# Where scores, turns and splits stand between the projections of a three-layer block (one core)

## The chip, the core and the metric

The kernel runs on one core of a Trainium2 chip. The core has five engines that work side by side: TensorE (PE) multiplies matrices into PSUM, VectorE (DVE) and ScalarE (ACT) work elementwise, GpSimd (POOL) too, SyncE (SP) issues DMAs. Each engine takes its own instructions strictly in order; between engines they wait on semaphores. The metric is the device time of one execution in microseconds.

## The reference

The input is 256 tokens of 1024 floats. `first_block` is a layer with two attentions over the same projection and a feed-forward; `second_block` has two layers, each with an attention, a mixture of 32 experts and a gated embedding. What matters here, cut:

```python
# first_block
proj = einsum(rms_norm(h), w_in); qa, ka, va, c_q, c_kv, k_rope = split(proj)
qa, ka = rms_norm(per head)                    # 8 heads of 64
out_a = dilated_attention(qa, ka, va, rel_bias)
qb = einsum(rms_norm(c_q), w_uq)               # 8 heads of 96, "latent" heads
kv = einsum(rms_norm(c_kv), w_ukv)             # keys' part and values
qb, kb = rms_norm(per head), then rope
out_b = causal_block_attention(qb, kb, vb)
h = h + concatenate([out_a, out_b]) @ w_o
h = h + square(relu(rms_norm(h) @ w_ff1)) @ w_ff2
# second_block, layer 0: nsa_attention (16 heads, with compressed blocks), experts, gate
# second_block, layer 1: moba_attention
k, v = split(rms_norm(h) @ w_kv_shared); k = rms_norm(k)        # 4 heads
q = rms_norm(rms_norm(h) @ w_q)                                 # 16 heads
o = softmax(q k + alibi) v; h = h + o @ w_out
h = h + hier_moe(rms_norm(h))
h = h + sigmoid(rms_norm(h) @ ple_w_gate) * (p @ ple_w_proj)    # the end
```

## The kernel before

**Tiling.** The 256 tokens are two tiles of 128 (`t`). All matrices are float32; a weight chunk is split into a rounded high part (ScalarE, `split`, line 906) and a low remainder (VectorE, line 909), and each product is three matmuls: high by high, high by low, low by high (`pe_linear`, line 888). A chunk has two of the eight 128-row blocks of a matrix, up to 512 columns wide. Four split chunks fit (`PAIRS`), so `take_linear` splits chunk n + 4 while TensorE works on chunk n; at the end of a column group it takes the result out of its bank (lines 933 to 937), with the normalization's factor.

**Order of work.** Nothing is scheduled by a planner: each engine's order is the order of the calls in its block (`@block.tensor`, `.scalar`, `.vector`, `.gpsimd`, `.sync`), written by hand. `pe_linear` has a hook, `ahead`, which issues other work before chunk c of its first group.

**A head's way.** A projection's result is squared (`squares`, ScalarE), summed (VectorE), a root is taken (`act_root`, ScalarE), refined by six short VectorE instructions (`dve_root`, lines 749 to 754), and the heads are scaled (`scale_heads`, line 957, on VectorE or GpSimd). TensorE turns them (`pe_turn`, line 792) and ScalarE and VectorE take the turned heads to SBUF (`take_turn`). Then `scores_of_pair` (line 970) scores two heads, VectorE adds mask or bias and finds the maximum (`bias_head`, 1090), ScalarE takes the exponential (`exps_of`, 1054), TensorE turns the probabilities (995), one of the two copies them, TensorE multiplies with the values (1006), and `mix_core` (1119) scales four heads at once. Banks 0 to 3 hold scores and projections, 4 and 5 turned probabilities, 6 and 7 values.

**Names.** `l_uq`, `l_ukv`, `l_va` are the projections of the latent queries, of the latent keys and values, and of the first attention's values; `t_a`, `t_b` the turns of the first and of the latent attention's heads (qa/ka and qb/kb); `att_a`, `att_b`, `att_n`, `att_m` the four attentions. Before the first matmul of `l_va` TensorE waits for `dve_scaled` 2, both scalings of the first attention's heads. The feed-forward (`pe_in` 1336, `pe_down` 1346) adds 32 units into four banks; `dve_units` then adds the banks to `h` (1438). In the last layer before: `l_q` (all 16 query heads), `l_k`, `l_v`, and after each half of the queries its squares, sum, root and scaling; `t_mq[0]`, `t_mq[1]`, `t_mk` are the turns of the query halves and the keys. The kernel ends with `l_gate[1]`, sigmoid (933), product and addition (1970, 1973), and two stores.

## Time and profile before

| | us |
|---|---|
| three runs | 1069.54, 1071.67, 1073.91 |
| their median | 1071.67 |
| the profiled execution | 1069.12 |
| its span, first to last instruction | 1067.3 |
| TensorE busy | 1016.9 (95%) |
| VectorE busy | 762.6 (71%) |
| ScalarE busy | 701.4 (66%) |
| GpSimd busy | 104.5 (10%) |
| mean granted TensorE clock | 0.994 |

Busy times overlap, since the engines work side by side. A timeline row gives the start in us from the span's start, the length of the merged instructions, engine, line and operation; in brackets stands how long the engine was idle before, and whose work ended that. The profiled execution is one execution, 0.2% below the median.

### The profile page before, as it was taken

What the parts mean: (1) busy time and instruction counts of PE and PEld (TensorE: products, weight loads), DVE (VectorE), ACT (ScalarE), POOL (GpSimd) and SP (SyncE); (2) the same over time, 40 slices, a digit from 0 to 9 for tenths busy, and PEclk for the clock granted to TensorE, in tenths of its full rate; (3) what the DMA queues carried; (4) which work ended last, traced back from release to release, by engine and by line L of the source; (5) the groups of instructions that cost most, each with busy time, mean ns of one, the idle gap of its engine ahead of it and who ended that gap; (6) DMA issues with size and microseconds to landing.
All of it is one profiled execution on the core that took longest, in us unless ns stands there. A gap on an engine that the chain in (4) does not pass through costs nothing.

```text
span 1067.3 us, 17403 instructions
## 1 busy us (share of the span) xinstructions
PE 1016.9 (95%) x6109; PEld 849.7 (80%) x6109; DVE 762.6 (71%) x1338; ACT 701.4 (66%) x1201; POOL 104.5 (10%) x194
## 2 busy tenths in 40 slices
PE   7997899999999999999899999999989999999998
PEld 6875878999998777887687877867878688877866
DVE  4686557666665675877668887887777668888876
ACT  5665535444444545765599898957576588899955
POOL 9008000000000100200510000000000330000000
PEclk9999999999999999999999999999999999999999
DMA  9972027666663557004449999854314429899941
GB/s 293 294 226 72 1 79 230 185 194 183 185 185 122 178 171 245 23 2 158 177 159 335 325 342 336 303 178 152 126 73 158 178 98 326 327 338 337 339 167 40
DMA packets 106157, 209.25 MB, mean 196 GB/s; under 512 B 7737, under 2 KB 51745, under 8 KB 105825
## 3 DMA queue, kind: packets, MB, share of 16 engines
q1 hardware_dynamic: 103584, 204.04, 56.0%
q0 software_dynamic: 2064, 3.25, 1.1%
q8 instruction: 43, 0.70, 0.3%
q10 hardware_dynamic: 432, 0.99, 0.3%
q14 instruction: 34, 0.27, 0.1%
HBM read 207.19 MB, written 1.06 MB: 195 GB/s over the span
## 4 chain that ended last, share of the span: by engine, by line
PE 84%; DVE 7%; ACT 4%; issue 2%; DMA 1%; SPq 0%; ACTq 0%; POOL 0%; DVEq 0%; POOLq 0%
PE bank L888 22%; PE bank L1663 18%; PE bank L1682 11%; PE bank L1336 8%; PE bank L1346 8%; PE bank L1006 4%; PE bank L970 2%; PE bank L792 2%; PE bank L995 2%; PE bank L1704 1%; PE bank L1531 1%; DMA ring<-in_a_w_in 1%; PE bank L1674 1%; PE bank L1493 1%; PE bank L2166 1%
## 5 line engine op out<-in xcount | busy, mean ns | idle before, releaser
L888 PE MATMUL bank<-weight_parts,x_high 128*128 128x512 f32 (+2 forms) x768 | 224.9, 377 | 8.6 <-ACT x_high L856 2.6
L1663 PE MATMUL bank<-expert_high,block_high 128*128 128x256 f32 x560 | 184.1, 329 | 3.4 <-ACT block_low L1611 2.4
L1591 DVE TENSOR_TENSOR expert_low<-expert_w,expert_high 128x1024 fp32r<-128x1024 f32 x140 | 164.7, 1219 | 6.9 <-ACT expert_high L1584 6.6
L888 PEld LDWEIGHTS bank<-weight_parts,x_high 128*128 128x128 f32 x768 | 139.9, 189 | 35.9 <-ACT x_high L856 7.0
L909 DVE TENSOR_TENSOR weight_parts<-ring,weight_parts 128x1024 fp32r<-128x1024 f32 (+3 forms) x112 | 122.1, 1110 | 51.9 <-ACT weight_parts L906 51.3
L1663 PE MATMUL bank<-expert_high,block_low 128*128 128x256 f32 x560 | 158.2, 282 | 0.0
L1663 PE MATMUL bank<-expert_low,block_high 128*128 128x256 f32 x560 | 158.0, 282 | 0.0
L906 ACT CAST weight_parts<-ring 128x1024 fp32r<-128x1024 f32 (+3 forms) x112 | 104.3, 956 | 78.0 <-PE bank L888 60.0
L1584 ACT CAST expert_high<-expert_w 128x1024 fp32r<-128x1024 f32 x140 | 140.1, 1052 | 17.1 <-DMA expert_w<-in_moe_w_up 16.5
L888 PE MATMUL bank<-weight_parts,x_low 128*128 128x512 f32 (+2 forms) x384 | 143.7, 374 | 0.0
L1682 PE MATMUL bank<-expert_w,junk 128*128 128x512 f32 x280 | 131.3, 592 | 0.0
L1663 PEld LDWEIGHTS bank<-expert_high,block_high 128*128 128x128 f32 x560 | 106.8, 191 | 19.6 <-issue 14.8
L1663 PEld LDWEIGHTS bank<-expert_low,block_high 128*128 128x128 f32 x560 | 106.8, 191 | 15.3 <-issue 15.3
L1663 PEld LDWEIGHTS bank<-expert_high,block_low 128*128 128x128 f32 x560 | 106.8, 191 | 0.0
L1336 PE MATMUL bank<-x_high,parts 128*128 128x256 f32 x512 | 97.5, 283 | 0.4 <-DVE x_low L858 0.3
L1346 PE MATMUL bank<-parts,hid_parts 128*128 128x512 f32 x384 | 92.9, 391 | 0.0
L1738 DVE SCALAR_TENSOR_TENSOR arena<-bank,home_w,arena 128x1024 f32 x64 | 82.2, 1284 | 9.1 <-issue 5.3
L1336 PEld LDWEIGHTS bank<-x_high,parts 128*128 128x128 f32 x512 | 82.1, 191 | 2.2 <-issue 0.7
L888 PEld LDWEIGHTS bank<-weight_parts,x_low 128*128 128x128 f32 x384 | 72.5, 189 | 12.9
L1346 PEld LDWEIGHTS bank<-parts,hid_parts 128*128 128x128 f32 x384 | 70.1, 188 | 13.3
L1682 PEld LDWEIGHTS bank<-expert_w,junk 128*128 128x128 f32 x280 | 47.7, 190 | 34.4 <-issue 34.4
L1609 ACT CAST block_high<-sorted_high 128x1024 fp32r (+1 forms) x70 | 73.4, 1051 | 1.8 <-issue 1.0
(362 smaller groups left out, 1683.4 us busy)
## 6 DMA issues: line engine op xcount, KB each, us to landing
expert_w<-in_moe_w_gate SPq DMA_DIRECT2D x70, 512.0 KB, 5.8
expert_w<-in_moe_w_up SPq DMA_DIRECT2D x70, 512.0 KB, 7.2
expert_w<-in_moe_w_down SPq DMA_DIRECT2D x70, 512.0 KB, 5.3
ring<-in_w_ff SPq DMA_DIRECT2D x64, 512.0 KB, 3.9
ring<-in_w_in SPq DMA_DIRECT2D x16, 512.0 KB, 8.1
ring<-in_a_w_in SPq DMA_DIRECT2D x16, 512.0 KB, 6.5
ring<-in_ple_w_gate SPq DMA_DIRECT2D x16, 512.0 KB, 5.6
ring<-in_w_o SPq DMA_DIRECT2D x8, 512.0 KB, 4.1
```

What stands on the lines that cost most here:

```text
L888: mm = nc.tensor.matmul(bank[:, j["m"] % 4, 0:n], j["operand"][x][:, 2 * c + kk, at[0]:at[1]], weight_parts[:, number % PAIRS, w, kk * n:( ...
L906: nc.scalar.copy(high, raw_weights).then_inc(weights_high, 1)
L909: nc.vector.tensor_tensor(low, raw_weights, high, ALU.subtract).then_inc(weights_split, 1)
L1006: mm = nc.tensor.matmul(bank[:, 6 + t, (n % 4) * P:(n % 4 + 1) * P], probT[:, n % 2, q * P:(q + 1) * P], v[:, kt, at - 64:at + 64], start= ...
L1336: mm = nc.tensor.matmul(bank[:, b, 0:256], parts[:, u % 2, w, k * P:(k + 1) * P], x[:, k, :], start=k == 0 and n == 0, stop=k == KB - 1 an ...
L1346: mm = nc.tensor.matmul(bank[:, 2 * t + half, :], hid_parts[:, u % 2, x, t * P:(t + 1) * P], parts[:, u % 2, w, 2048 + half * 512:2048 + ( ...
L1584: nc.scalar.copy(half_of(expert_high[:, b % 2, :], j), half_of(expert_w[:, b % DEPTH, 0:2048], j)).then_inc(ex_cast, 1)
L1591: nc.vector.tensor_tensor(half_of(expert_low[:, b % DEPTH, 0:2048], j), half_of(expert_w[:, b % DEPTH, 0:2048], j), half_of(expert_high[:, ...
L1609: nc.scalar.copy(block_high[:, b % 2], sorted_high[:, :, ds(at, P)]).then_inc(ex_copied, 1)
L1663: mm = nc.tensor.matmul(bank[:, 4 + b % 2, 0:256].rearrange("p (q n) -> p q n", q=2), x[:, b % 2, k, :], w[:, k], start=k == 0 and n == 0, ...
L1682: mm = nc.tensor.matmul(bank[:, 2 * (b % 2) + half, :], hidTs[:, b % 2, :], expert_w[:, b % DEPTH, 2048 + half * 512:2048 + (half + 1) * 5 ...
L1738: v.scalar_tensor_tensor(out=here, in0=bank[:, 2 * (b % 2):2 * (b % 2) + 2, :].rearrange("p b n -> p (b n)"), scalar=share_of, in1=here, o ...
```

## The change

1. **First attention.** `t_a` is still turned before chunk 2 of `l_va`; the first pair of heads is now scored before chunk 3, and VectorE adds the biases of the first two heads before it takes `l_va`. VectorE does the splits and the taking of `l_uq[2:]` ahead of the scaling of qa, and those of `l_ukv[:2]` ahead of the scaling of ka. The latent queries' root is taken earlier, ahead of the turns.
2. **All attentions by four.** The start is written out anew, with scores in pairs, each pair waiting for its own two banks.
3. **Latent attention.** Heads are turned pair by pair, queries and keys alternating; the first two jobs stand ahead of the wait for the mix, and scores wait for their own pair.
4. **Feed-forward end.** VectorE adds the first token tile once `first_tile_down` is there, which the last unit's first six matmuls set.
5. **Compressed attention.** VectorE inverts the gates ahead of taking the compressed scores.
6. **Last layer's projections.** Order: first half of the queries (`l_mq0`), keys, second half (`l_mq1`), values; turns and first scores stand inside the values' projection, the turn of the second half inside the attention's start.
7. **End.** The last gate projection's second half is two groups of 256 columns; the output goes in six stores.

The diff, cut:

```diff
+        if halved_end:
+            wide += [256, wide.pop() - 256]
...
-    t_b = turn_heads(vb_q, 8, qbT, None) + turn_heads(vb_k, 8, kbT, None)
+    t_b = [job for i in range(0, 8, 2) for view, dest in ((vb_q, qbT), (vb_k, kbT))
+           for job in turn_heads(view[:, :, i:i + 2], 2, dest[:, i:i + 2], None)]
...
-    l_q = linear(a["b_w_q_2"][0], KB, D_MODEL, x_parts, moba_q, "copy", n_moba)
     t_kv = turn(h, KB, [(kv_high, gains["kv_norm"], kv_low)])
+    l_mq0 = linear(a["b_w_q_2"][0], KB, 512, x_parts, moba_q, "copy", n_moba, at=0)
     l_k = linear(a["w_kv_shared_2"], KB, 256, (kv_high, kv_low), moba_kv, "copy", n_moba, at=0)
+    l_mq1 = linear(a["b_w_q_2"][0], KB, 512, x_parts, moba_q, "copy", n_moba, at=512)
     l_v = linear(a["w_kv_shared_2"], KB, 256, (kv_high, kv_low), moba_kv, "copy", n_moba, at=256)
-    run(l_q + l_k + l_v)
-    r_mq = [root(16, DIM), root(16, DIM)]
-    r_mk = root(8, DIM)
+    run(l_mq0 + l_k + l_mq1 + l_v)
...
-        if n >= 4:
-            pe.wait_ge(biased, n)
-        scores_of_pair(pe, n, four[0:2])
-        scores_of_pair(pe, n + 2, four[2:4])
-
-    def pe_attention(pe, s, compressed=False, by_four=False, before_values=None, scored=2):
+        for pair in (0, 2):
+            if n >= 4:
+                pe.wait_ge(biased, n + pair - 2)
+            scores_of_pair(pe, n + pair, four[pair:pair + 2])
...
+                    if j % 2 == 0:
+                        wait_turned(pe, turned_by[j:j + 2])
...
+        if free is not None:
+            turn_probs(first)
+            free()
         if scored == 2:
             scores_of_pair(pe, first + 2, here[2:4])
-        turn_probs(first)
-        for j in range(len(here)):
+        if free is None:
+            turn_probs(first)
+        pe.wait_ge(biased, first + 2)
+        scores_of_pair(pe, first + 4, here[4:6])
+        turn_probs(first + 1)
+        if between is not None:
+            between()
+        pe.wait_ge(biased, first + 4)
+        scores_of_pair(pe, first + 6, here[6:8])
+        if before_values is not None:
+            before_values()
+        values(first, here[0])
+        for j in range(1, len(here)):
             if j % 4 == 0 and j + 4 < len(here):
                 scores_of_four(pe, first + j + 4, here[j + 4:j + 8])
             if j + 1 < len(here):
                 turn_probs(first + j + 1)
             if compressed and j == len(here) - 2:
                 pe_turn_compressed(pe)
-            if j == 0 and before_values is not None:
-                before_values()
             values(first + j, here[j])
...
+            if u == UNITS - 1 and t == 0:
+                mm.then_inc(first_tile_down, 1)
...
-        dve.wait_ge(down_made, OPEN + UNITS)
-        for t in range(TILES):
+        for t in range(TILES):
+            if t == 0:
+                dve.wait_ge(first_tile_down, 1)
+            else:
+                dve.wait_ge(down_made, OPEN + UNITS)
...
-            sp.wait_ge(ple_done, 7 + t)
-            sp.dma_start(out[0, t * P:(t + 1) * P, :], h[:, t, :]).then_inc(stored, 16)
-        sp.wait_ge(stored, 32)
+        for done, cols in ((5, slice(0, 512)), (7, slice(512, 768)), (9, slice(768, 1024))):
+            for t in range(TILES):
+                sp.wait_ge(ple_done, done + t)
+                sp.dma_start(out[0, t * P:(t + 1) * P, cols], h[:, t, cols]).then_inc(stored, 16)
+        sp.wait_ge(stored, 96)
...
+        def first_pair_of_a():
+            wait_turned(pe, t_a)
+            wait_took(pe, l_ukv)
+            scores_of_pair(pe, att_a["first"], att_a["heads"][0:2])
+
+        pe_linear(pe, l_va, ahead={2: lambda: pe_turn(pe, t_a), 3: first_pair_of_a})
         wait_took(pe, l_va)
-        scores_of_pair(pe, att_a["first"], att_a["heads"][0:2])
         pe_attention(pe, att_a, by_four=True)
         pe.wait_ge(pool_scaled, 2)
         pe.wait_ge(*probT_of(att_b["first"] - 1))
         pe.wait_ge(*probT_of(att_b["first"] - 2))
+        pe_turn(pe, t_b[:2])
         pe.wait_ge(mixed, att_b["first"] // 4)
-        pe_turn(pe, t_b)
-        wait_turned(pe, t_b)
-        pe_attention(pe, att_b)
+        pe_turn(pe, t_b[2:])
+        pe_attention(pe, att_b, turned_by=t_b)
...
-        pe_linear(pe, l_q[0:2], t_moba)
-        pe_turn(pe, t_kv)
-        pe_linear(pe, l_q[2:4])
+        pe_linear(pe, l_mq0, t_moba, ahead={2: lambda: pe_turn(pe, t_kv)})
         pe_linear(pe, l_k, t_kv)
-        pe.wait_ge(dve_scaled, 4)
-        pe_linear(pe, l_v, ahead={2: lambda: pe_turn(pe, t_mq[0])})
-        pe.wait_ge(dve_scaled, 5)
-        pe_turn(pe, t_mq[1])
-        pe.wait_ge(pool_scaled, 5)
-        pe_turn(pe, t_mk)
-        wait_turned(pe, t_mk + t_mq[0] + t_mq[1])
-        wait_took(pe, l_v)
-        scores_of_pair(pe, att_m["first"], att_m["heads"][0:2])
-        pe_attention(pe, att_m, by_four=True)
+
+        def turn_keys_of_m():
+            pe.wait_ge(pool_scaled, 5)
+            pe_turn(pe, t_mk)
+
+        def turn_first_heads():
+            pe.wait_ge(dve_scaled, 4)
+            pe_turn(pe, t_mq0)
+
+        def first_pair_of_m():
+            wait_turned(pe, t_mk + t_mq0)
+            wait_took(pe, l_mq1)
+            scores_of_pair(pe, att_m["first"], att_m["heads"][0:2])
+
+        def turn_last_heads():
+            pe.wait_ge(dve_scaled, 5)
+            pe_turn(pe, t_mq1)
+
+        pe_linear(pe, l_mq1)
+        pe_linear(pe, l_v, ahead={1: turn_keys_of_m, 2: turn_first_heads, 3: first_pair_of_m})
+        pe_attention(pe, att_m, by_four=True, between=turn_last_heads, before_values=lambda: wait_turned(pe, t_mq1),
+                     free=lambda: wait_took(pe, l_v))
...
+        take_linear(dve, l_uq[2:], "dve")
         dve.wait_ge(scale_ready, 1)
         scale_heads(v, qa, scales(r_a, 0, 8), dve_scaled)
-        take_linear(dve, l_uq[2:], "dve")
+        take_linear(dve, l_ukv[:2], "dve")
         scale_heads(v, ka, scales(r_a, 8, 8), dve_scaled)
+        take_linear(dve, l_ukv[2:], "dve")
         dve.wait_ge(squared, 2)
         v.tensor_reduce(r_bq["sum"], flat_mix[:, 0:1536].rearrange("p (h d) -> p h d", d=96), AX.X,
                         ALU.add).then_inc(sums_ready, 1)
-        take_linear(dve, l_ukv, "dve")
+        dve_root(dve, r_bq, scale_ready)
         take_turn(dve, t_a, "dve")
         dve_latent_sums(dve)
+        dve.wait_ge(toep_ready, 32)
+        for i in range(2):
+            bias_head(dve, att_a["first"] + i, att_a["heads"][i])
         take_linear(dve, l_va, "dve")
-        dve_root(dve, r_bq, scale_ready)
+        for i in range(2, 4):
+            bias_head(dve, att_a["first"] + i, att_a["heads"][i])
         dve_root(dve, r_bk, scale_ready)
-        dve.wait_ge(toep_ready, 32)
-        dve_attention(dve, att_a, by_four=True)
+        dve_attention(dve, att_a, by_four=True, begun=4)
...
+        take_linear(dve, l_k, "dve", between={2: scale_first_half})
+        dve.wait_ge(squared, 8)
         v.tensor_reduce(r_mk["sum"], work[:, 0:512].rearrange("p (h d) -> p h d", d=64), AX.X,
                         ALU.add).then_inc(sums_ready, 1)
         dve_root(dve, r_mk, scale_ready)
-        take_turn(dve, t_mq[0], "dve")
+        take_linear(dve, l_mq1, "dve")
+        take_turn(dve, t_mk, "dve")
+        dve.wait_ge(squared, 9)
+        v.tensor_reduce(r_mq1["sum"], rows[:, 1, :].rearrange("p (h d) -> p h d", d=64), AX.X,
+                        ALU.add).then_inc(sums_ready, 1)
+        take_turn(dve, t_mq0, "dve")
+        dve_root(dve, r_mq1, scale_ready)
+        for i in range(2):
+            bias_head(dve, att_m["first"] + i, att_m["heads"][i])
+        dve.wait_ge(scale_ready, 8)
+        steepen(r_mq1, 8, 8)
         take_linear(dve, l_v, "dve")
-        take_turn(dve, t_mq[1], "dve")
-        take_turn(dve, t_mk, "dve")
-        dve_attention(dve, att_m, by_four=True)
+        scale_heads(v, mq[:, :, 8:16, :], scales(r_mq1, 0, 8), dve_scaled)
+        for i in range(2, 4):
+            bias_head(dve, att_m["first"] + i, att_m["heads"][i])
+        dve_attention(dve, att_m, by_four=True, begun=4, later=lambda: take_turn(dve, t_mq1, "dve"))
```

What it moves, as the programs list it. VectorE ahead of the values' projection of the first attention (`weight_parts_49` are the split weights, `ring` the raw ones; `arena` holds the projection, `stat` the roots). Before, then now:

```order
L957 TENSOR_TENSOR arena<-arena,stat 128x512 [waits scale_ready]
L957 TENSOR_TENSOR arena<-arena,stat 128x512
L909 TENSOR_TENSOR weight_parts_49<-ring,weight_parts_49 128x1024 [waits weights_high] x3
L937 TENSOR_SCALAR arena<-bank,stat 128x256 [waits rooted,lin_made]
L957 TENSOR_TENSOR arena<-arena,stat 128x512 x2
L2493 TENSOR_REDUCE stat<-mix 128x16 [waits squared]
L909 TENSOR_TENSOR weight_parts_49<-ring,weight_parts_49 128x1024 [waits weights_high]
L937 TENSOR_SCALAR second<-bank,stat 128x512 [waits rooted,lin_made]
```

```order
L914 TENSOR_TENSOR weight_parts_49<-ring,weight_parts_49 128x1024 [waits weights_high] x3
L944 TENSOR_SCALAR arena<-bank,stat 128x256 [waits rooted,lin_made]
L964 TENSOR_TENSOR arena<-arena,stat 128x512 [waits scale_ready]
L964 TENSOR_TENSOR arena<-arena,stat 128x512
L914 TENSOR_TENSOR weight_parts_49<-ring,weight_parts_49 128x1024 [waits weights_high]
L944 TENSOR_SCALAR second<-bank,stat 128x512 [waits rooted,lin_made]
L964 TENSOR_TENSOR arena<-arena,stat 128x512 x2
L914 TENSOR_TENSOR weight_parts_49<-ring,weight_parts_49 128x1024 [waits weights_high]
```

The scaling of the queries moved behind three splits and a take, that of the keys behind a fourth split and a second take; the sum over `mix` comes later still.

TensorE at the start of the last attention (`kv_high`, `kv_low` are the keys' and values' input, `ring` the turned heads, `work` the probabilities, `arena` the heads to be turned). Before, from the turns behind the last chunk of `l_v`:

```order
L792 MATMUL bank<-table,arena 128x128 [waits dve_turned,act_turned,dve_scaled]
L792 MATMUL bank<-table,arena 128x128 x3
L792 MATMUL bank<-table,arena 128x128 [waits dve_turned,pool_scaled]
L970 MATMUL bank<-ring 128x128 [waits act_took,dve_took,dve_turned,act_turned]
L970 MATMUL bank<-ring 128x256 x2
L995 MATMUL bank<-table,work 128x128 [waits act_probT,probs_made]
L970 MATMUL bank<-ring 128x128 [waits biased]
L995 MATMUL bank<-table,work 128x128 [waits dve_probT,probs_made]
L1006 MATMUL bank<-arena,probT 128x128 [waits mixed,act_probT]
```

And now, from the first scores, ahead of the last chunk:

```order
L977 MATMUL bank<-ring 128x128 [waits act_took,dve_took,dve_turned,act_turned]
L977 MATMUL bank<-ring 128x256 x2
L893 MATMUL bank<-weight_parts_49,kv_high_57 128x256 [waits weights_split]
L1002 MATMUL bank<-table,work 128x128 [waits act_probT,probs_made]
L977 MATMUL bank<-ring 128x128 [waits dve_took,act_took]
L977 MATMUL bank<-ring 128x128 [waits biased]
L1002 MATMUL bank<-table,work 128x128 [waits dve_probT,probs_made]
L797 MATMUL bank<-table,arena 128x128 [waits dve_turned,act_turned,dve_scaled]
L977 MATMUL bank<-ring 128x128 [waits biased]
L1013 MATMUL bank<-arena,probT 128x128 [waits act_probT,mixed,dve_turned,act_turned]
```

The first scores moved in front of a chunk of the values' projection, the keys' turns (which wait for `pool_scaled`) three chunks ahead, and the last turns (those that wait for `dve_scaled`) behind three pairs of scores.

## Rows read from the trace of the kernel before

**Rows 1.** The page, chain of waits by engine.

```profile
PE 84%; DVE 7%; ACT 4%; issue 2%; DMA 1%; SPq 0%; ACTq 0%; POOL 0%; DVEq 0%; POOLq 0%
```

**Rows 2.** TensorE's waits, 60 to 96.5; columns: engine, line, releaser, total, times, longest.

```profile
PE bank L888 <- ACT second L935: 1.5, 1, 1.5
PE bank L888 <- DVE arena L937: 1.0, 1, 1.0
```

**Rows 3.** VectorE's timeline; columns: start, us, engine, line, operation.

```profile
75.11 3.49 DVE L909 TENSOR_TENSOR weight_parts<-ring,weight_parts 128x1024 fp32r<-128x1024 f32 x3
78.51 0.48 DVE L937 TENSOR_SCALAR arena<-bank,stat 128x256 f32<-128x256 f32 x1
78.91 1.28 DVE L957 TENSOR_TENSOR arena<-arena,stat 128x512 f32<-128x512 f32 x2
```

**Rows 4.** ScalarE's timeline, the same stretch.

```profile
79.07 1.49 ACT L2248 ACTIVATE mix<-arena 128x1536 f32<-128x1536 f32 x1 [3.51 <-issue]
80.47 1.03 ACT L906 CAST weight_parts<-ring 128x1024 fp32r<-128x1024 f32 x1
```

**Rows 5.** TensorE's timeline, values' projection and start of the first attention.

```profile
82.22 0.70 PE L888 MATMUL bank<-weight_parts,x_high 128*128 128x512 f32 x2 [1.52 <-ACT second L935]
...
84.40 0.73 PE L888 MATMUL bank<-weight_parts,x_high 128*128 128x512 f32 x2 [0.55 <-DVE second L937]
...
96.95 1.58 PE L970 MATMUL bank<-ring 64*128 64x128 f32 x16 [0.99 <-DVE arena L937]
102.12 0.55 PE L995 MATMUL bank<-table,work 128*128 128x128 f32 x3 [3.59 <-ACT work L1054]
...
105.92 1.19 PE L1006 MATMUL bank<-arena,probT 128*128 128x128 f32 x6
```

**Rows 6.** Windows of 2 us; the third number from the end is the granted clock.

```profile
102.00:104.00 2.00, 1.78 (x13) 1.39 (x15) 0.71 (x6) 2.00 (x10) 2.00 (x3) 0.81 0.04 8
104.00:106.00 2.00, 2.00 (x13) 1.35 (x11) 0.64 (x4) 1.94 (x9) 2.00 (x2) 0.50 0.00 0
...
784.00:786.00 2.00, 1.60 (x10) 0.88 (x9) 1.92 (x13) 1.37 (x7) 0.00 (x0) 0.52 0.00 0
```

**Rows 7.** Timelines of GpSimd and of VectorE, the same moment.

```profile
96.08 2.50 POOL L2071 TENSOR_TENSOR arena<-second,gain_bk 128x512 f32<-128x512 f32 x2
...
97.42 1.20 DVE L751 TENSOR_TENSOR stat<-stat 128x16 f32<-128x16 f32 x1
```

**Rows 8.** TensorE's timeline, start of the latent attention.

```profile
115.92 3.67 PE L792 MATMUL bank<-table,arena 128*96 128x128 f32 x32 [1.06 <-DVE mix L1119]
120.42 0.46 PE L986 MATMUL bank<-ring 96*128 96x128 f32 x2 [0.83 <-ACT ring L833]
```

**Rows 9.** Timelines of TensorE and of VectorE, end of the feed-forward.

```profile
338.56 5.63 PE L1346 MATMUL bank<-parts,hid_parts 128*128 128x512 f32 x24
345.76 1.16 PE L781 MATMUL bank<-table,h 128*128 128x128 f32 x8 [1.57 <-DVE h L1438]
...
344.30 2.73 DVE L1438 SCALAR_TENSOR_TENSOR h<-bank,stat,h 128x512 f32<-128x512 f32 x4 [1.80 <-PE bank L1346]
```

**Rows 10.** TensorE's waits, 770 to 810.

```profile
PE bank L970 <- ACT ring L814: 1.7, 1, 1.7
...
PE bank L792 <- POOL arena L957: 0.7, 1, 0.7
...
PE bank L888 <- issue: 0.5, 1, 0.5
PE bank L995 <- ACT work L1054: 0.4, 1, 0.4
```

**Rows 11.** The chain in order of time; columns: start, us, what, count.

```profile
172.87 2.87 PE bank L1336 x24
...
1040.04 20.70 PE bank L888 x90
```

**Rows 12.** DMA issues, the stores; columns: count, KB each, median us to landing.

```profile
out<-h SPq DMA_DIRECT2D x2, 512.0 KB, 2.7
```

More of the change, by code:

```diff
@@ L915, in split_first, with take_linear @@
             split(eng, number, engine)
-    def take_linear(eng, jobs, engine):
+    def take_linear(eng, jobs, engine, between=None):
         for group in zip(jobs[0::2], jobs[1::2]):
-            for number in group[0]["splits"]:
+            for c, number in enumerate(group[0]["splits"]):
+                if between is not None and group[0] is jobs[0] and c in between:
+                    between[c]()
                 if number + PAIRS <= group[0]["end"]:
```

113 lines of the change are left out of this document (60 added, 53 removed).

## The prediction

> **What bounds the kernel now.** I read the page's chain of waits first: it runs over TensorE for 84% of the span [rows 1], so nothing that only relieves another engine pays; what can be won is a stretch in which TensorE stands idle or has its lower clock. Second I asked whom TensorE waits for, stretch by stretch, around the places that the change touches. Ahead of the values' projection there are waits of 1.5 and 1.0 us [rows 2]. At the start of the first attention it idles 0.99 and 3.59 us, and the first values start at 105.92 [rows 5]. The latent attention starts with 32 turns of 3.67 us and a wait of 0.83 [rows 8]; behind the feed-forward it waits 1.57 us [rows 9]; around the start of the last attention 1.7, 0.7, 0.5 and 0.4 us [rows 10]. Third, the granted clock in windows of 2 us: 0.81 and 0.50 behind the gap of 3.59, and 0.52 in 784 to 786, behind the waits of the last attention [rows 6]; 0.50 is 1.2 GHz instead of 2.4. As TensorE is the bound before and behind every gap, what is won at one is kept to the end.
>
> The sums are made against the profiled execution, 1069.12 us (span 1067.3 and 1.82 around it).
>
> **Part 1, head of the values' projection (a loss).** Before, VectorE splits three chunks of weights (3.49 us, 1.16 each), takes the latent queries at 78.51 and scales the keys from 78.91 to 80.2 [rows 3]. Now these splits and the take stand ahead of the scaling of the queries (1.3 us): the take comes at 77.4, ScalarE's squares, which wait for it, start at 77.9 instead of 79.07, and its next cast at 79.4 instead of 80.47 [rows 4]. But the scaling of the keys now stands behind the fourth split and a further take, and that split waits for that cast: cast done 80.4, split 81.6, take (0.7) 82.3, scaling (1.3) 83.6. TensorE waits for both scalings before its first matmul of the values, in both kernels. So it starts at 83.6 instead of 82.22; its second tile, which waited again and started at 84.40 [rows 5], has its bank by then and starts at 83.6 + 1.4 = 85.0. Cost +0.6 us.
>
> Behind this wait lies a second cost. TensorE now stands idle from 79.3 to 83.6, 4.3 us. Idle of 0.99 and 3.59 us was followed by a stretch at half clock [rows 5, 6], and waits of 0.7 and 1.7 us with little work between them by another [rows 6, 10]; the waits of rows 2, with matmuls of 1.4 us between them, by none. I take a stretch as behind the 3.59 us, some 3.2 us long (2 us whole, parts on both sides), half of which is lost: +1.6 us, bounds 0 and 1.7. The Trainium skill, in "TensorE: Matmul & The Clock Gate" (the HAM clock gate), says that the slow state is the default and activity releases it; by it the loss would be certain and the sum as below, and this trace agrees with it at both gaps. If the clock stayed up, that is rival (a).
>
> **Part 2, first attention.** One pair of scores (half of 1.58 us [rows 5], 0.8) moves in front of the last chunk of the values' projection, and two heads' additions run on VectorE under that chunk. Walked from 85.0 as if the clock were full: the second tile of the first chunk, three chunks of 2.73, the turns (1.7) and the pair end at 97.1; the last tile is taken by 97.85; then pair, turn, pair, turn, pair (0.8, 0.33, 0.8, 0.33, 0.8) and the first values at 100.95, where they stood at 105.92 [rows 5]. Without part 1's 0.6 that is -5.6; I take -5.4. It is made of the gaps of 0.99 and 3.59 and of the 1.5 us that the half clock took there, less the new wait of 0.8. ScalarE keeps up: exponentials of a head are 0.9 us and can start at 97.2. The second root (six short instructions, 1.2 us) now stands among the heads' additions and can hold the second head's values once: +0.4 (0 to 1.2). GpSimd's last scaling then ends at 107.1, before it is wanted at 110.
>
> **Part 3, latent attention.** Before, turns and wait fill 115.92 to 120.42 [rows 8], behind a wait of 1.1 us for the mix. Now the first pair of queries and keys is turned under that wait, six jobs follow (2.6 us with their banks), and the first scores need only the first pair: 2.7 us from the mix instead of 4.7. -2.1 us (-1 to -2.8).
>
> **Part 4, end of the feed-forward.** The last unit's second token tile is 6 of the 24 matmuls of 5.63 us [rows 9], 1.4 us, so the first tile's sums are whole at 342.8. VectorE's four additions (2.73 us) started at 344.30. Two of them now run from 342.9, TensorE's first turn starts at once at 344.3 (345.76 before), and the last addition ends at 345.7 instead of 347.0. -1.3 us (-1.2 to -1.4).
>
> **Part 5, compressed attention.** Scores by pairs of banks, and the gates ahead of the compressed scores: no wait above 0.3 us stands there to be won. 0 (-0.5 to 0).
>
> **Part 6, last attention.** The four waits are 3.3 us [rows 10], the half clock some 1.5 [rows 6]: 4.8 at most. In the new order the second half of the queries (11 us of matmuls) and the values (5.8) stand beside the roots, scalings and turns of the rest. Tightest place: the second half's first chunk of weights. Behind the first half's take come squares (1.1), the sum (1.2) and beside it the cast (1.03) and split (1.16): ready at 759.9, wanted at 760.0. Next: the keys' scaling on GpSimd, ready at 770.9, wanted at 772.4. Then the first pair is scored by 777.8, the projection ends at 779.2, the first exponentials at 779.3, and the last heads' turns lie between scores. First values at 783.7, before at 788.4. I take -4.5 us (-4.8 to -1).
>
> **Part 7, end.** A matmul of 256 columns takes 2.87/24 = 0.12 us and one of 512 20.7/90 = 0.23 [rows 11]; the last 48 become 96 narrow ones: 11.5 instead of 10.9, +0.6. Between the two new pieces TensorE waits some 0.4, as VectorE's gate instructions stand ahead of the next split. Behind the last matmul the narrow gate work is 0.7 shorter. The last store is 128 KB instead of 512; that landed in 2.7 us [rows 12], 1.3 of them bytes at the 400 GB/s seen then, so a quarter gives 1.7, -1.0. Sum -0.7, bounds -1.2 and +0.5; I take -0.6. By "DMA: Bandwidth & Descriptors" of the Trainium skill (anatomy of one DMA: about 2.0 us fixed) the small store would land in 2.3, an estimate, and this sum would be 0.
>
> **Sum.** +0.6 +1.6 -5.4 +0.4 -2.1 -1.3 +0 -4.5 -0.6 = -11.3 us: 1057.8 against 1069.12. The median of the three timed runs is 1071.67; less 11.3 it gives 1060.4. The profiled time lies below all three, so I lean to the median but not wholly: 1059.5.
>
> **Rivals.** (a) The clock stays up at the values' head: -12.9, 1058. For it the waits of rows 2, after which it stayed; against, two gaps after which it fell. (b) A wait inside a projection. TensorE takes its work in order, so a turn or pair put inside and not ready holds the rest. For it the margin of 0.1 us in part 6; against, 1.5 us at the keys. Part 6 wins 1 instead of 4.5 and part 2 one less: -6.8, 1064. (c) Waits are only moved: parts 2, 3 and 6 win a third, 4 of 12: -3.3, 1067.5. For it: VectorE and ScalarE release nearly all these gaps, and no work is taken off them. Against: both stand idle for microseconds in the same stretches. (d) Slower: GpSimd and VectorE hold each other up. A tiny VectorE instruction took 1.20 us, with its like at 0.2, beside a GpSimd one of 2.50 [rows 7]. The latent queries' root (6), the keys' scaling (2) and the second root (6) now fall beside GpSimd's rotations and scalings: 14 instructions by 1.0 us are +14; if GpSimd's own scaling stretches too, the latent turns wait 7 more: -11.3 + 21 = +10, 1081. It passes the old time from about 12 caught instructions; of the twelve root instructions before the first attention one was caught.
>
> **How the numbers follow.** Forecast 0.60, (a) 0.15, (b) 0.13, (c) 0.09, (d) 0.03. Faster by over 0.5% (5.4 us, about what a measurement of this kernel can tell from no change) are the first three, 0.88; within it (c), 0.09; slower (d), 0.03. The range reaches from (a) with the costs at their good ends, 1055, over (b) to just short of (c), 1067.
>
> **What would show it.** Part 1: about 4 us idle before the first matmul of the values and a window at 0.5 behind it. Part 2: no gap over 1 us from there to the first values, which start near 102.5 with the half clock. Part 3: first latent scores 2.7 us behind the mix. Part 4: the first turn after the feed-forward without a wait. Part 6: full clock and no wait over 0.5 us up to the first values of the last attention. Part 7: the last store landing in under 2 us. A wait of several microseconds inside a projection, or more than two or three VectorE instructions at 1 us beside GpSimd, would make the forecast wrong.

## The result, and the profile after

| | before | now |
|---|---|---|
| median of four runs, us | 1071.74 | 1063.43 (1062.75 to 1065.02) |
| ratio | | 0.9925, interval 0.9901 to 0.9948 |
| profiled execution, us (span) | 1069.12 (1067.3) | 1062.88 (1061.1) |
| the changed kernel once more, ten runs (E4), beside fifteen of before | 1070.96 | 1064.99; ratio 0.9949, 0.9933 to 0.9965 |

The kernel is faster by 6 to 8 us; 12.2 were forecast (1059.5), with 1055 to 1067 as the range. The time lies where rival (b) was priced (1064), but that mechanism is not in the trace.

The page's chain of waits, by engine, has TensorE at 85% where it had 84% [rows 1]:

```profile
PE 85%; DVE 6%; ACT 4%; issue 3%; DMA 2%; SPq 0%; ACTq 0%; DVEq 0%
```

TensorE's timeline at the values' projection, against [rows 5]:

```profile
82.73 1.22 PE L893 MATMUL bank<-weight_parts,x_high 128*128 128x512 f32 x2 [5.17 <-DVE arena L964]
...
87.96 0.63 PE L893 MATMUL bank<-weight_parts,x_high 128*128 128x512 f32 x2
...
100.12 0.93 PE L977 MATMUL bank<-ring 64*128 64x128 f32 x8 [0.94 <-DVE arena L944]
100.98 0.55 PE L1002 MATMUL bank<-table,work 128*128 128x128 f32 x3
...
102.31 0.55 PE L1002 MATMUL bank<-table,work 128*128 128x128 f32 x3
103.64 0.60 PE L1013 MATMUL bank<-arena,probT 128*128 128x128 f32 x3
```

The gap of 3.59 us is gone, and there is one of 5.17 us ahead of the projection: part 1. Two matmuls take 1.22 us there and 0.63 five microseconds later; the windows (third number from the end is the granted clock) say why:

```profile
82.00:84.00 2.00, 1.27 (x3) 1.09 (x4) 2.00 (x3) 0.00 (x0) 1.92 (x3) 0.50 0.66 247
84.00:86.00 2.00, 2.00 (x6) 1.54 (x6) 2.00 (x3) 1.17 (x3) 1.92 (x3) 0.50 0.31 40
86.00:88.00 2.00, 2.00 (x7) 1.59 (x6) 1.52 (x5) 0.43 (x2) 1.92 (x4) 0.53 0.59 222
```

Why 5.17 and not 4.3: VectorE's timeline, then GpSimd's, against [rows 3]:

```profile
78.38 2.15 DVE L914 TENSOR_TENSOR weight_parts<-ring,weight_parts 128x1024 fp32r<-128x1024 f32 x1 [1.33 <-ACT weight_parts L911]
80.45 0.74 DVE L944 TENSOR_SCALAR second<-bank,stat 128x512 f32<-128x512 f32 x1
81.12 1.56 DVE L964 TENSOR_TENSOR arena<-arena,stat 128x512 f32<-128x512 f32 x2
```

```profile
77.64 1.80 POOL L2093 TENSOR_TENSOR arena<-arena,gain_bq 128x768 f32<-128x768 f32 x1 [20.53 <-ACT mix L2294]
79.53 1.32 POOL L2085 TENSOR_TENSOR rows<-arena,rope 128x128 f32<-128x128 f32 x1
```

The split that took 1.16 us before takes 2.15 beside GpSimd's multiplication, whose end it seems to wait for (79.44; 1.09 us are left from there). The scalings take 1.56 instead of 1.28.

TensorE, start of the latent attention, against [rows 8]. The mix's last scaling ends at 113.14, so the first scores (115.86) come 2.7 us behind it, as forecast:

```profile
112.17 3.85 PE L797 MATMUL bank<-table,arena 128*96 128x128 f32 x32
115.86 0.39 PE L993 MATMUL bank<-ring 96*128 96x128 f32 x2
```

Behind the feed-forward 0.21 us are left of the wait of 1.57 [rows 9]:

```profile
339.74 1.16 PE L786 MATMUL bank<-table,h 128*128 128x128 f32 x8 [0.21 <-DVE h L1468]
```

TensorE's waits, 755 to 790, against [rows 10] (total, times, longest), and the DMA issues at the end, against [rows 12] (count, KB each, median us to landing):

```profile
PE bank L977 <- ACT ring L838: 0.5, 1, 0.5
PE bank L1002 <- ACT work L1075: 0.2, 1, 0.2
```

```profile
out<-h SPq DMA_DIRECT2D x2, 256.0 KB, 2.0
out<-h SPq DMA_DIRECT2D x4, 128.0 KB, 1.7
```

Three differences of the two profiles lie where nothing was changed. The first projection's matmuls ran at half clock up to 14.4 us before and at full clock now (1.8 us for the new one); this is read from their lengths, 0.63 us for a single one against 0.39, as the granted clock of those windows reads 1.00 in both profiles. From where TensorE starts the routing of an expert layer (L1478, now L1508) to the first matmul with `place` it took 14.7 us before in both layers, and takes 16.1 now, with a half-clock stretch of 6 to 7 us. Here the first layer's:

```profile
508.00:510.00 2.00, 2.00 (x9) 1.93 (x10) 1.23 (x7) 1.97 (x3) 0.00 (x0) 0.50 1.02 418
510.00:512.00 2.00, 2.00 (x3) 0.67 (x2) 1.69 (x10) 1.72 (x2) 0.00 (x0) 0.50 1.05 424
512.00:514.00 2.00, 2.00 (x4) 0.81 (x3) 1.73 (x9) 0.58 (x1) 0.00 (x0) 0.50 1.02 406
```

### The profile page after: what moved, and what is told of

It reads as the page before. It is cut to its first block, busy times and chain, and to the rows that moved or that the text cites. A ratio compares the mean times of both kernels' runs of the same rounds, so it can differ in the third digit from the quotient of the medians.

```text
span 1061.1 us, 17535 instructions
## 1 busy us (share of the span) xinstructions
PE 1021.5 (96%) x6157; PEld 853.4 (80%) x6157; DVE 764.5 (72%) x1346; ACT 701.5 (66%) x1207; POOL 106.4 (10%) x194
## 4 chain that ended last, share of the span: by engine, by line
PE 85%; DVE 6%; ACT 4%; issue 3%; DMA 2%; SPq 0%; ACTq 0%; DVEq 0%
PE bank L893 23%; PE bank L1693 17%; PE bank L1712 10%; PE bank L1361 8%; PE bank L1371 8%; PE bank L1013 4%; PE bank L797 2%; PE bank L1002 2%; PE bank L977 2%; PE bank L1523 1%; PE bank L1734 1%; PE bank L1508 1%; PE bank L1561 1%; DMA ring<-in_a_w_in 1%; PE bank L1704 1%
## 5 line engine op out<-in xcount | busy, mean ns | idle before, releaser
L893 PE MATMUL bank<-weight_parts,x_high 128*128 128x512 f32 (+3 forms) x800 | 227.4, 370 | 12.5 <-DVE arena L964 5.2
L893 PEld LDWEIGHTS bank<-weight_parts,x_high 128*128 128x128 f32 x800 | 144.3, 190 | 39.0 <-ACT x_high L861 7.0
L893 PE MATMUL bank<-weight_parts,x_low 128*128 128x512 f32 (+3 forms) x400 | 146.9, 367 | 0.0
L893 PEld LDWEIGHTS bank<-weight_parts,x_low 128*128 128x128 f32 x400 | 75.8, 190 | 12.4
```

Source lines behind the costliest of these rows:

```text
L893: mm = nc.tensor.matmul(bank[:, j["m"] % 4, 0:n], j["operand"][x][:, 2 * c + kk, at[0]:at[1]], weight_parts[:, number % PAIRS, w, kk * n:( ...
```

## The experiments

Each kernel is an edit of the changed kernel. Stretches are read between marks of the same execution: the first projection's tenth low matmul, called the start mark (what the clock did at the start, which differs from profile to profile, lies ahead of it), the first values of the first attention, and so on. "First values" is the first matmul of probabilities with values, "first scores" the first one of queries with keys.

**E1, scalings where they were.**

```diff
-        take_linear(dve, l_uq[2:], "dve")
         dve.wait_ge(scale_ready, 1)
         scale_heads(v, qa, scales(r_a, 0, 8), dve_scaled)
-        take_linear(dve, l_ukv[:2], "dve")
+        take_linear(dve, l_uq[2:], "dve")
         scale_heads(v, ka, scales(r_a, 8, 8), dve_scaled)
-        take_linear(dve, l_ukv[2:], "dve")
+        take_linear(dve, l_ukv, "dve")
```

> The changed kernel, but VectorE scales the first attention's queries and keys where the kernel before did: qa ahead of the splits and the take of l_uq[2:], ka ahead of the takes of l_ukv. My theory: the gap of 5.17 us ahead of the values' projection is the order on VectorE (and 0.95 of it GpSimd's neighbourhood), and the half clock behind it follows from the gap. Then the gap shrinks to 2 to 3 us, the two waits of 0.3 and 1 us of the latent projections come back (+1.3), and the time falls by 1 us if the half clock stays and by 3.5 if it goes. Rival, the half clock is chance and has nothing to do with the gap: it may stay or go, and the start of the first values moves by 1 us only. Rival, the gap is made by ScalarE's take of the bank and not by the scalings: nothing changes.

Measured: 1059.94 us (0.9892 of before, 0.9865 to 0.9919), 5.0 below the changed kernel in the same group. TensorE's timeline:

```profile
77.13 0.73 PE L893 MATMUL bank<-weight_parts,ckv_high 128*128 128x512 f32 x2 [1.01 <-DVE arena L944]
80.31 0.70 PE L893 MATMUL bank<-weight_parts,x_high 128*128 128x512 f32 x2 [1.52 <-ACT second L942]
...
99.61 0.60 PE L1013 MATMUL bank<-arena,probT 128*128 128x128 f32 x3
```

The wait of 1.0 us came back, the gap shrank to 1.52 us, and no window from 80 to 420 us is below full clock. The first values come 4.0 us earlier, 3.9 from the start mark: the whole price of part 1. From the projection's start to the first values 19.30 us pass, 20.91 in the changed kernel and 23.70 before. The gain of 5.0 in time is more than I gave at most (3.5). At the site this is because the stretch at half clock was dearer than 1.6. But 3.0 of the 3.9 are lost again at the compressed attention, which runs at half clock in this profile, and the profiled execution is only 2.2 and 2.7 us below the two of the changed kernel (1060.71 against 1062.88 and 1063.43); why the medians lie 5.0 apart is not shown.

**E2, the wait for the scalings at the turn.**

```diff
-        pe.wait_ge(dve_scaled, 2)
+        def turn_heads_of_a():
+            pe.wait_ge(dve_scaled, 2)
+            pe_turn(pe, t_a)
...
-        pe_linear(pe, l_va, ahead={2: lambda: pe_turn(pe, t_a), 3: first_pair_of_a})
+        pe_linear(pe, l_va, ahead={2: turn_heads_of_a, 3: first_pair_of_a})
```

> The changed kernel, with TensorE's wait for both scalings moved from before the values' projection into the turn of the heads, ahead of its third chunk: the first two chunks need only their weights and banks. My theory: the scalings alone hold the projection back. TensorE then starts at about 79 instead of 82.7 (the bank is taken at 78.9), the gap is 1.4 us and the half clock (2.5 us) goes; about 5 us are won at the projection's third chunk, of which VectorE, which takes the turned heads only behind the root of the latent queries (about 89), gives back 1: -4 us. Rival, waits are only moved: TensorE then stands as long ahead of the turn or of the first pair as it stood ahead of the projection, and the time falls by 1 us or less.

Measured: 1061.31 us (0.9913, 0.9888 to 0.9939).

```profile
79.12 0.70 PE L893 MATMUL bank<-weight_parts,x_high 128*128 128x512 f32 x2 [1.51 <-ACT second L942]
...
91.06 0.93 PE L977 MATMUL bank<-ring 64*128 64x128 f32 x8 [0.90 <-issue]
...
99.43 0.82 PE L1013 MATMUL bank<-arena,probT 128*128 128x128 f32 x5
```

As expected to 0.2 us: start at 79.1, 0.90 us given back at the pair, first values 4.2 us earlier. The rival, that waits are only moved, falls at this site. But where the first routing starts, at 504 us, only 1.2 of the 4.2 are left, as the compressed attention ran at half clock (E10).

**E3, GpSimd held.**

```diff
         wait_took(pool, l_uq)
+        pool.wait_ge(dve_scaled, 2)
```

> The changed kernel, with GpSimd's work on the latent heads held back until VectorE has scaled the first attention's heads. My theory: GpSimd slows VectorE while both work: the split that took 2.15 us takes 1.2 and the scalings 1.28 instead of 1.56, the gap ahead of the values' projection is 3.9 to 4.2 us instead of 5.17, the half clock stays, and the time falls by 1 us. GpSimd ends its rotations and gains at about 101 instead of 96, still before the second root at 103.4, so the latent attention is not later. Rival: these instructions are long for another reason (the ScalarE cast ahead of them, a DMA): the split stays at 2 us, the time is the same. Rival: the two engines collide later instead (roots among the heads' additions at 1 us each): the time is the same or 1 us longer.

Measured: 1062.03 us (0.9919, 0.9895 to 0.9943). VectorE, then TensorE:

```profile
78.39 1.23 DVE L914 TENSOR_TENSOR weight_parts<-ring,weight_parts 128x1024 fp32r<-128x1024 f32 x1 [1.33 <-ACT weight_parts L911]
79.54 0.74 DVE L944 TENSOR_SCALAR second<-bank,stat 128x512 f32<-128x512 f32 x1
80.20 1.28 DVE L964 TENSOR_TENSOR arena<-arena,stat 128x512 f32<-128x512 f32 x2
```

```profile
81.53 1.22 PE L893 MATMUL bank<-weight_parts,x_high 128*128 128x512 f32 x2 [3.96 <-DVE arena L964]
```

The same split takes 1.23 instead of 2.15 us: GpSimd cost 1.2 us of the gap. Behind 3.96 us of idle the clock still falls, but for a shorter stretch; the first values come 2.3 us earlier. In time it is 3.0 us below the changed kernel of the same group, where I expected 1: the shorter half clock, 1.1 of the 2.3, was not in my sum.

**E4, the changed kernel once more.**

> The changed kernel once more, unaltered. In the first profile its matmuls ran at full clock from the start (those of the kernel before at half clock up to 14.4 us, a difference of 1.8 us), and the routing of both expert layers ran some 7 us at half clock (the kernel before: none in the first, 4 us in the second; 1.4 us each). If these are chance, this profile shows other ones of them; if the change causes them by its shifted times, the same ones come again. The half clock behind the gap at 82.7 should come again in either case.

Measured: 1064.99 us (0.9949, 0.9933 to 0.9965). Half clock up to 15 us this time; the gap of 5.16 us and the stretch behind it came again; the first routing took 16.1 us again, the second 14.7 instead of 16.1. So the start differs between executions of one kernel, the head does not; for the routing see E10 to E12.

**E5, E2 and E3 together.**

> Both edits together: TensorE waits for the scalings only ahead of the turn, and GpSimd starts behind them. The theory says that they add where they meet: with the wait late, TensorE's second tile waits for VectorE's take (0.56 us) and the first pair for the turned heads (0.90 us, VectorE's chain of split, take, scaling, sum and root); with GpSimd held this chain is 1.2 us shorter, so both waits go and the first values come 1 to 1.5 us earlier than with the late wait alone, at about 98.2. Behind it a stretch at half clock at 422 to 430, as in the three kernels before that came there 2 to 4 us earlier than the changed kernel, gives 3 us back. So 1 us below the late wait alone. Rival: GpSimd, started later, holds the roots of the latent queries instead: same time as the late wait alone.

Measured: 1060.35 us (0.9910, 0.9887 to 0.9934). From the start mark the first values come 1.7 us before those of the late wait alone, but most of it is lost again behind them, as in the rival though at another root. VectorE, GpSimd and TensorE:

```profile
98.01 0.78 DVE L755 TENSOR_SCALAR stat<-stat 128x16 f32<-128x16 f32 x1
98.83 1.20 DVE L756 TENSOR_TENSOR stat<-stat 128x16 f32<-128x16 f32 x1
```

```profile
97.50 2.50 POOL L2104 TENSOR_TENSOR arena<-second,gain_bk 128x512 f32<-128x512 f32 x2
```

```profile
101.77 0.94 PE L1013 MATMUL bank<-arena,probT 128*128 128x128 f32 x6 [1.30 <-DVE probT L1123]
```

Two instructions of the second root, whose like take 0.17 us, take 2.0 us until GpSimd ends at 100.0, and TensorE waits 1.30 us: the mechanism of rival (d), with two instructions caught. At the latent scores 0.1 us is left of the 1.7.

**E6, the last attention's order as before.** The edit puts back `l_q`, `l_k`, `l_v` with their turns, roots and takes; the start of the attentions by pairs stays.

> The changed kernel with the last layer's projections, turns and scores in the order of before (the last attention's start by pairs stays). My theory: this part is worth what the first profile shows between the start of the last layer and its first values, 3.75 us, of which 1.5 are a stretch at half clock that the short waits brought. So +3.7 us, with waits of 1.7, 0.7, 0.5 us and a window at 0.5 at 775 to 785; without the half clock +2.3. Rival, the gain there is given back in the routing that follows (half clock 2 us longer in the changed kernel than before): +2 us or less at the end of the routing.

Measured: 1066.58 us (0.9974, 0.9960 to 0.9987). Waits, 755 to 790:

```profile
PE bank L976 <- ACT ring L818: 1.7, 1, 1.7
PE bank L1001 <- ACT work L1074: 1.1, 1, 1.1
PE bank L796 <- POOL arena L963: 0.7, 1, 0.7
PE bank L892 <- issue: 0.5, 1, 0.5
```

From the start of the last layer to its first values 46.16 us instead of 43.12: part 6 is worth 3.0 us here, without any half clock, where I expected 2.3 for that case. Where the clock stayed up, TensorE waited 1.1 us for the exponentials instead of 0.4 [rows 10]. The half clock of [rows 6] thus cost before 0.7 us (46.87), and 0.8 against E12, not 1.5. In time it is 2.6 us above E8, which ran beside it and differs from the changed kernel only at the end. The rival is seen too: the second routing takes 14.7 us here and 16.1 in E8, so that behind it 1.9 us of the difference are left (2.8 against E4, which took 14.7).

**E7, latent turns and feed-forward end as before.** The edit restores `t_b = turn_heads(vb_q, ...) + turn_heads(vb_k, ...)`, its one wait, and `dve.wait_ge(down_made, OPEN + UNITS)` ahead of all four additions.

> The changed kernel with the latent heads turned as before (all 32 turns behind the mix, then all waited for) and the feed-forward's end in one piece. Their trace sites are far from the others. Theory: +2.1 (1.9 to 2.3) from the mix to the first latent scores, +1.36 at the first turn behind the feed-forward, +3.4 us together at 340 us. Rival: from there on the compressed attention's start sees the time shifted by 3.4 us later, which in the profiles so far was the side on which it keeps full clock, so nothing more is lost there; if the shift itself decides the clock, the whole difference may come out at 3.4 to 0.5.

Measured: 1067.39 us (0.9974, 0.9958 to 0.9990).

```profile
114.82 3.67 PE L796 MATMUL bank<-table,arena 128*96 128x128 f32 x32 [1.06 <-DVE mix L1141]
119.31 0.46 PE L992 MATMUL bank<-ring 96*128 96x128 f32 x2 [0.83 <-ACT ring L837]
```

```profile
344.63 1.16 PE L785 MATMUL bank<-table,h 128*128 128x128 f32 x8 [1.57 <-DVE h L1464]
```

From the first values to the latent scores 14.24 us instead of 12.22 (2.0), and 1.36 at the feed-forward: both terms stand. Its profiled execution was only 2.0 us above E4's: the first routing took 14.7 us instead of 16.1, without half clock.

**E8, wide last group, four stores.** `halved_end` off; stores of 512 columns as soon as each half is whole.

> The changed kernel with the last gate projection in two groups of 512 columns as before, but four stores of 256 KB, the first two as soon as the first half is whole. Theory: the two halves of part 7 cancel. TensorE ends 1.0 us earlier (0.6 of narrow matmuls, 0.4 of the wait ahead of the split), the gate's work behind the last matmul is 0.9 longer, and the last store lands in 2.0 us (as the two of 256 KB did) instead of 1.7: within 0.5 us of the changed kernel. Rival: the finer end is worth its 1 us: +1.

Measured: 1063.98 us (0.9941, 0.9918 to 0.9963). From the last gate's first matmul to the end of the span: 27.26 and 27.31 us in the two profiles of before, 26.97 now, 26.63 here. All eleven profiles with the new end lie between 26.94 and 27.00. So part 7 wins 0.3 us (bounds -1.2 and +0.5), and stores by column halves alone 0.6 to 0.7; the narrow matmuls cost more than they bring.

**E9, second root before the take.** On top of E5:

```diff
+        dve_root(dve, r_bk, scale_ready)
         take_linear(dve, l_va, "dve")
         for i in range(2, 4):
             bias_head(dve, att_a["first"] + i, att_a["heads"][i])
-        dve_root(dve, r_bk, scale_ready)
```

> Late wait and GpSimd held, and the second latent root taken on VectorE before it takes the values' projection (VectorE stands idle there for 1.2 us), instead of between the additions of heads 3, 4 and 5, where two of its six short instructions took 0.78 and 1.20 us beside GpSimd's scaling of 2.50 and TensorE then waited 1.30 us. Theory: that wait goes and the root's 1.2 us with it; 1.3 us earlier at the latent attention than with the two edits alone, start clock aside. In time 0 to 1.3 less, as the half clock at 422 to 430 comes in either case. Rival: the root now delays the take of the projection and the pair behind it by as much: same.

Measured: 1059.78 us (0.9894, 0.9867 to 0.9921). The wait of 1.30 us is gone; from the start mark the latent scores come 1.55 us earlier than in E5, 1.7 than in E2 and 5.9 than in the changed kernel. Half clock from 423 to 430 took 3.0 us back at the compressed attention. E1 and E9 are the fastest, 11 us below before in their groups, where the changed kernel was 6 below; the two can't be told apart, and both beat both kernels.

**E10 and E11, the same work, later.** In E2 (20 matmuls) and in the changed kernel (24):

```diff
+        for _ in range(5):        # E11: 6
+            for q in range(4):
+                nc.tensor.matmul(bank[:, q, :], zeros[0:32, 0:P], zeros[0:32, :], start=True, ...)
         pe_clear(pe, 0)
```

> The kernel with the late wait, with 20 extra matmuls of zeros (32 x 512, on banks that are cleared next) ahead of the feed-forward, about 4.5 us of TensorE work that changes nothing else. The late wait reached the first scores of the compressed attention at 417.6 us and ran at half clock from 422 on, losing 2.9 us; the changed kernel came at 421.9 and kept full clock. Theory (the clock depends on when a light stretch comes): now it comes at 422 and keeps full clock, so of 4.5 us added only 1.6 are left behind that attention, and in the time +1.5 or less against the late wait. Rival (the half clock belongs to the edited program, or to what VectorE and ScalarE do): the stretch stays and the time is +4.5.

> The changed kernel with 24 such matmuls, some 5.4 us. It then reaches the first routing when the kernel before did, which had no half clock there (the changed kernel had 7 us of it, a loss of 1.0 to 1.4). Theory: that stretch goes, and 4.0 to 4.4 of the 5.4 us are left. Rival: the half clock in the routing belongs to the changed program: it stays and 5.4 are left.

Measured: 1067.17 us (0.9970) and 1071.76 us (1.0024). The times missed (E10 is 5.9 us above E2, where the theory said 1.5 at most and the rival 4.5), because the added matmuls lengthen the way from the latent scores to the end of the feed-forward by 8.3 and 7.6 us instead of 4.5 and 5.4: they bring a half clock of their own. E11's ten executions spread from 1067.84 to 1077.76, so its time decides nothing. At the two places the clock did what the theory said. E10's windows, at the added matmuls and at the compressed attention, and under them E2's at the latter:

```profile
158.00:160.00 2.00, 2.00 (x6) 1.49 (x6) 0.97 (x1) 0.00 (x0) 0.00 (x0) 0.50 0.33 103
160.00:162.00 2.00, 2.00 (x7) 1.25 (x6) 0.00 (x0) 0.00 (x0) 0.00 (x0) 0.50 1.09 347
...
428.00:430.00 2.00, 2.00 (x21) 2.00 (x20) 1.97 (x12) 2.00 (x12) 1.18 (x2) 1.00 0.00 0
430.00:432.00 2.00, 2.00 (x21) 1.80 (x21) 1.41 (x2) 0.95 (x5) 0.87 (x1) 1.00 0.00 0
```

```profile
422.00:424.00 2.00, 2.00 (x13) 1.75 (x12) 1.02 (x2) 0.39 (x2) 0.73 (x1) 0.60 0.03 8
424.00:426.00 2.00, 2.00 (x11) 1.27 (x11) 0.49 (x4) 1.36 (x5) 1.20 (x2) 0.50 0.00 0
426.00:428.00 2.00, 2.00 (x11) 1.09 (x9) 1.51 (x9) 0.99 (x4) 0.00 (x0) 0.50 0.00 0
```

E10 reaches that attention 8.1 us later than E2 and the first routing 5.0 later. E11's first routing takes 14.7 us, without half clock. So at both places the same code, reached later, kept its clock, and the half clock does not belong to the edited program alone. That the time of arrival sets it rests on one profile for each place.

**E12, before once more.**

> The kernel before once more, unaltered. If the clock at a given place follows the time of arrival, its half-clock stretches come again at 103 to 107, 782 to 786 and in the second routing, none at 424 to 430 and none in the first routing; only the start (half clock up to 14.4 us or none) is free, and shifts all by up to 1.9 us. If they are chance, other ones are seen.

Measured: 1070.14 us (0.9998, 0.9985 to 1.0011). Windows at the first attention, the last one and the first routing:

```profile
102.00:104.00 2.00, 2.00 (x13) 1.35 (x10) 0.64 (x4) 2.00 (x9) 2.00 (x2) 0.50 0.00 0
784.00:786.00 2.00, 0.83 (x9) 0.33 (x5) 1.93 (x14) 1.71 (x8) 0.00 (x0) 1.00 0.00 0
...
522.00:524.00 2.00, 2.00 (x3) 0.67 (x2) 1.97 (x4) 0.58 (x1) 1.76 (x4) 0.50 0.00 0
```

The stretch behind the idle 3.59 us came again. The one in the last attention did not (46.07 us there instead of 46.87); TensorE waits 1.1 us for the exponentials there, as in E6:

```profile
PE bank L995 <- ACT work L1054: 1.1, 1, 1.1
```

The first routing had one (15.8 us), reached 1.7 us earlier than in the first profile of before. So one program has its half clock at different places from execution to execution. The last attention's first scores came at 782.69 and at 782.40, 0.3 us apart, and the clock differed: there the time of arrival, as far as it was read, does not separate the two.

## Why the prediction was right, and where its sum was off

The start mark and the other marks are those of the experiments.

| part | forecast | measured | from |
|---|---|---|---|
| 1, head | +2.2 | +3.9 | start mark to first values, now against E1 |
| 2, first attention | -5.0 | -4.4 | the same marks, E1 against before |
| 3, latent | -2.1 | -2.0 to -2.3 | first values to latent scores |
| 4, feed-forward end | -1.3 | -1.4 | wait at 339.74; E7 |
| 5, compressed | 0 | +0.3 | first scores to first values, 7.93 against 7.64 |
| 6, last attention | -4.5 | -3.0 to -3.8 | layer start to first values, 43.1 against 46.1 and 46.9 |
| 7, end | -0.6 | -0.3 | gate's start to the end of the span |
| sum | -11.3 | -7 to -8 | |

The direction, the order of the gains and the loss at the head were right. Parts 3 and 4 were read from a chain with one releaser and are right to 0.2 us.

The step that failed is part 1, "so it starts at 83.6 instead of 82.22", with "+1.6 us" for the clock. Against the start mark TensorE started 2.3 us later, not 1.4: I added the bare durations of split, take and scaling, though GpSimd's work on the latent queries, let go by the earlier take, now lies beside them. I had put this neighbour into rival (d) and priced it only for short instructions. E3 shows 1.2 us for it, the half-clock stretch aside, and its start is 1.1 us later than before's, near the 1.4 of the sum. The Trainium skill, in "SBUF — State Buffer" (SBUF: two separate sides), says that VectorE with two inputs from SBUF and GpSimd hold a shared pair of ports in turn, each for a whole instruction; 2.15 us beside GpSimd, 1.23 without, and the split's last 1.09 us behind GpSimd's end agree. And the half clock lasted 5.2 us, not 3.2: the matmuls from 82.73 to 87.96 take 2.9 us in E1, without the 0.8 that its second tile comes late there, so 2.4 were lost where I took 1.6. That the second tile no longer comes late was in the +0.6, and held.

In part 6 I took the half clock as lost time on top of the waits. It was mostly hidden: where TensorE runs faster it waits 0.7 us longer for ScalarE (1.1 us in E6 and E12, 0.4 before). In part 2 the root cost nothing, as forecast at the lower bound; the walk was some tenths short in several places: the pair takes 0.93 us for 0.8, and from the second pair to the first values 3.5 us pass for 3.1.

Rival (a) is refuted: behind 5.17 us of idle the clock fell in each profile of this order. (b) is refuted though its time fits: the longest wait inside a projection is 0.45 us, at the first pair of the last attention. (c) is refuted by E2, E6 and E7. (d) took 1.2 us at the head and 1.3 in E5, far from its price. In part 7 the landing of 1.7 us came as forecast from the rows. The 2.3 us that followed from the fixed part of about 2.0 us in the Trainium skill, "DMA: Bandwidth & Descriptors" (anatomy of one DMA), was too long, and the measurement decides; the page fits that figure to DMAs of GpSimd's queue, and these stores are SyncE's.

The two profiles differ by 6.2 us, the parts give 7.9. Clock at places without an edit makes -1.8 at the start and +2.8 in the two routings. A further +0.3 is a longer wait of TensorE ahead of the projection behind the last attention, here before and now:

```profile
811.37 0.70 PE L888 MATMUL bank<-weight_parts,x_high 128*128 128x512 f32 x2 [0.18 <-issue]
...
803.77 0.70 PE L893 MATMUL bank<-weight_parts,x_high 128*128 128x512 f32 x2 [0.52 <-issue]
```

It comes at full clock, with 0.52 to 0.54 us in all twelve profiles with the new start of the attentions and 0.18 in both of before, so it belongs to the changed program and not to the clock. Its cause was not looked for, and the sum had no term for it. That leaves 0.4 unassigned. That the runs gained 8.3 in one group and 6.0 in the other is not settled further; each profiled execution has its own set of half-clock stretches.

The prediction's premise that "what is won at one is kept to the end" did not hold. The routing, in which no term of the sum stood, takes 1.4 us back in E7's comparison, and the compressed attention takes 3 us back in the variants with a faster head. For the forecast itself these chances nearly cancel (-1.8 and +2.8), and the parts alone give 1063.8 to 1064.8 against the median of before, inside the range: that the time lies there is no luck. That it lies at rival (b)'s 1064 is.

## What to carry to other kernels

When a step is moved ahead so that a waiting engine is served sooner, look at what else that step releases: here an earlier take let GpSimd loose beside the very chain that TensorE waited for. Put a wait at the first instruction that needs it, not at the head of the phase (E2: one moved line, 4.2 us at the site). A gain of 4 us at one site can come out as 1 us further on (E2): read stretches between marks of one execution, and don't judge a site by the total.

## What was not expected of the hardware

- **A fall of the clock behind a short gap, by arrival.** The compressed attention starts alike in all profiles: TensorE idles 0.91 us (0.94 in E7), scores two pairs of heads (on 64 partitions), and runs 32 matmuls of 32 columns (3.76 us). In these fourteen profiles the time at which its first scores come separates those that lose clock from those that do not:

| first scores at, us | profiles | clock behind | first scores to first values |
|---|---|---|---|
| 417.6, 417.8, 418.6, 418.9, 419.7 | E2, E1, E9, E5, E3 | half | 10.5, 11.0, 11.0, 9.3, 9.5 |
| 421.9 to 431.0 | now, E8, E4, E6, E10, E12, E7, before, E11 | full | 7.9 (7.6 in the order of before) |

The five of the first row all have an edit at the head; E10 has E2's and stands in the second row.

- The first routing takes 14.7 us when reached by 504.9 (with 4 us at half clock, hidden by what VectorE has to do there), 16.1 from 505.0 to 506.9, 15.8 at 508.9 and 509.1, and 14.7 from 510.3 on. The five profiles reached by 504.9 are also the five that had half clock in the compressed attention, so time and history are not kept apart there (E9 at 504.90 takes 14.7, the changed kernel at 505.03 takes 16.1). In the second routing the same three durations occur without such an order. What sets them is open.
- TensorE can be busy in the trace all the time and still lose its clock: in E10 the matmuls on 32 partitions run from 153.0 us on, the granted clock is 1.00 in 152 to 154, 0.92 in 154 to 156 and 0.50 from 156 to 164, and TensorE is busy 2.00 of 2.00 us in each of these windows. The Trainium skill, in "TensorE: Matmul & The Clock Gate" (HAM oscillation), speaks of idle gaps; here there was none, and ahead of the falls in the compressed attention and in the routing of the changed kernel none over 1 us.
